# Splitting GpSimd's preparation of a state-space group into two separately ordered steps

## What is computed

```python
def ssd_chunked(x, dt, a, bm, cm):            # 8 groups, 4 heads each, head width 64, state 128
    xdt = x * dt[..., None]
    adt = dt * a ; a_cs = cumsum(adt)
    cb = einsum('bclgn,bcsgn->bcgls', cm, bm)                     # scores of a group
    y_diag = einsum('bcgls,bcgrls,bcsgrp->bclgrp', cb, segsum_exp(adt), xdt)
    ...                                        # the state carries what lies in earlier chunks
def mamba2_mixer(proj, ...):
    z, xbc, dt = split(proj)
    xbc = silu(causal_depthwise_conv(xbc))     # x rows, B and C
    y = ssd_chunked(x, dt, a, B, C) + d_skip * x
    return rmsnorm(y * silu(z))                # by group of 256 columns
```

## Time and profile before

| | |
|---|---|
| three runs, us | 1820.11, 1821.31, 1822.19 (median 1821.31) |
| profiled execution, us | 1821.69 |
| its span, us | 1819.7 |
| granted TensorE clock | 0.998 |
| first state-space layer's groups | about 88 to 300 us of the span |
| second state-space layer's groups | about 1369 to 1581 us |
| table loads of ScalarE | 23, 1.28 us each |

### The profile page before, as it was taken

One profiled execution on the slowest core, in us unless ns is written; L12 is line 12 of the kernel. 1 busy time (PEld: TensorE's weight loads), 2 busy tenths in 40 slices (PEclk: granted clock), 3 DMA queues, 4 the chain that ended last, 5 costly groups with the idle time before them and its releaser, 6 DMA issues.

```text
span 1819.7 us, 25828 instructions
## 1 busy us (share of the span) xinstructions
PE 1792.5 (99%) x9572; PEld 1534.4 (84%) x9572; DVE 1159.0 (64%) x1466; ACT 1000.1 (55%) x1601; POOL 316.3 (17%) x615
## 2 busy tenths in 40 slices
PE   7999999999999999999999999999999999999999
PEld 5999878888887778888888888888899987888887
DVE  5777765566565655566566545655677886556555
ACT  6666764454455666554455645444566666545443
POOL 3443450000003131000001400000144355000000
PEclk9999999999999999999999999999999999999999
DMA  6544434555555433465556445665554443365563
GB/s 230 172 149 153 140 116 139 185 183 189 191 181 183 154 125 126 152 190 193 194 181 214 157 133 176 196 190 190 181 170 152 149 150 128 116 197 184 187 191 131
DMA packets 85272, 305.63 MB, mean 168 GB/s; under 512 B 9632, under 2 KB 11040, under 8 KB 85152
## 3 DMA queue, kind: packets, MB, share of 16 engines
q1 hardware_dynamic: 84576, 302.88, 51.1%
q10 hardware_dynamic: 576, 1.12, 0.2%
HBM read 302.91 MB, written 1.05 MB: 167 GB/s over the span
## 4 chain that ended last, share of the span: by engine, by line
PE 95%; ACT 2%; DVE 2%; issue 1%; DMA 0%; ACTq 0%; DVEq 0%
PE ps L1135 18%; PE ps L1137 18%; PE ps L1136 18%; PE ps L1157 13%; PE ps L1159 7%; PE ps L1146 3%; PE ps L1148 3%; PE ps L1147 3%; PE ps L1291 2%; PE ps L1241 2%; PE ps L1311 2%; PE ps L1175 1%; PE ps L1183 1%; ACT w_hi_t L1336 0%; DVE w_lo_t L1566 0%
## 5 line engine op out<-in xcount | busy, mean ns | idle before, releaser
L1566 DVE TENSOR_TENSOR w_lo_t<-raw,w_hi_t 128x1024 fp32r<-128x1024 f32 x570 | 704.9, 1245 | 465.5 <-ACT w_hi_t L1336 464.1
L1336 ACT ACTIVATE w_hi_t<-raw 128x1024 fp32r<-128x1024 f32 x570 | 598.1, 1059 | 410.3 <-PE ps L1137 162.4
L1157 PE MATMUL ps<-hT,w_hi_t 128*128 128x512 f32 x1024 | 361.6, 397 | 0.0
L1135 PE MATMUL ps<-w_hi_t,act_hi 128*128 128x512 f32 x832 | 328.6, 395 | 0.0
L1137 PE MATMUL ps<-w_hi_t,act_lo 128*128 128x512 f32 x832 | 324.6, 390 | 0.0
L1136 PE MATMUL ps<-w_lo_t,act_hi 128*128 128x512 f32 x832 | 324.0, 389 | 0.0
L1159 PE MATMUL ps<-hT,w_lo_t 128*128 128x256 f32 x1024 | 287.3, 281 | 0.0
L1157 PEld LDWEIGHTS ps<-hT,w_hi_t 128*128 128x128 f32 x1024 | 192.2, 188 | 46.2
L1159 PEld LDWEIGHTS ps<-hT,w_lo_t 128*128 128x128 f32 x1024 | 193.4, 189 | 1.1
L1137 PEld LDWEIGHTS ps<-w_hi_t,act_lo 128*128 128x128 f32 x832 | 156.2, 188 | 33.7
L1135 PEld LDWEIGHTS ps<-w_hi_t,act_hi 128*128 128x128 f32 x832 | 156.2, 188 | 32.1
(11 more groups left out here) (212 smaller groups left out, 2436.5 us busy)
## 6 DMA issues: line engine op xcount, KB each, us to landing
raw<-in_wstream SPq DMA_DIRECT2D x570, 512.0 KB, 3.5
mix<-in_mem SPq DMA_DIRECT2D x4, 256.0 KB, 5.2
x<-in_x SPq DMA_DIRECT2D x1, 1024.0 KB, 9.0
wsT<-in_sgu_wT ACTq DMA_DIRECT2D x1, 512.0 KB, 4.6
sgain<-in_sgu_gain ACTq DMA_DIRECT2D x1, 512.0 KB, 5.6
out<-x SPq DMA_DIRECT2D x1, 512.0 KB, 2.8
out<-x SPq DMA_DIRECT2D x2, 256.0 KB, 2.0
consts_sb<-in_consts SPq DMA_DIRECT2D x1, 384.0 KB, 10.5
```

Of the source, the lines that this page charges most:

```text
L1135: pe.matmul(o, ah, wh[:, n], start=first and c == 0, stop=False)
L1157: pe.matmul(o.rearrange("p (a b) -> p a b", a=2), wh[:, n], hT2[:, :, kt, :], start=first and c == 0, stop=False, skip_group_check=True)
L1336: act.activation(w_hi_t[:, u % RING, :], raw[:, u % RING, :], ACT.Copy).then_inc(w_hi, 1)
L1566: dve.tensor_tensor(w_lo_t[:, u % RING, :], raw[:, u % RING, :], w_hi_t[:, u % RING, :].bitcast(F32), ALU.subtract)\
```

## The change

ssd_prep becomes two steps. ssd_mv makes the masked decays. It waits in the plan for the decay step only, no more for the x rows, and is spawned with no delay right after the previous group's ssd_a. ssd_xd makes the weighed rows. It waits in the plan for the x rows, for ssd_mv of its own group and for ssd_xd of the group before. ssd_a of a group asks for its ssd_mv, ssd_m for its ssd_xd. GpSimd's operations are the same.

```diff
@@ COST
-    "ssd_prep": (0, 0, 0), ...
+    "ssd_mv": (0, 0, 0), "ssd_xd": (0, 0, 0), ...
@@ Plan.ssm
-        def prepare(g, done):
-            while g // 2 not in xs_act or self.decay_act is None:
+        def masked(g, done):
+
+            while self.decay_act is None:
                 yield 1
-            self.step("ssd_prep", g=g, l=l, n=l * SG + g, xs=xs_act[g // 2], done=done)
-            ready[g] = True
+            self.step("ssd_mv", g=g, l=l, n=l * SG + g, done=done)
+            ready["mv", g] = True
+
+        def weighted(g):
+            while g // 2 not in xs_act or ("mv", g) not in ready or (g and ("xd", g - 1) not in ready):
+                yield 1
+            self.step("ssd_xd", g=g, l=l, n=l * SG + g, xs=xs_act[g // 2])
+            ready["xd", g] = True
         ready = {}
 
         def groups():
-            yield from prepare(0, 0)
+            yield from masked(0, 0)
+            self.spawn(weighted(0))
             for g in range(SG):
                 n = l * SG + g
                 yield 1, "ssd_a"
-                while g not in ready or 16 + g // 4 * 4 not in conv or 24 + g // 4 * 4 not in conv:
+                while ("mv", g) not in ready or 16 + g // 4 * 4 not in conv or 24 + g // 4 * 4 not in conv:
                     yield 1
...
                 if g + 1 < SG:
-                    self.spawn(prepare(g + 1, jobs["S", 1].done), 1)
+                    self.spawn(masked(g + 1, jobs["S", 1].done))
+                    self.spawn(weighted(g + 1), 1)
                 yield 1, "ssd_m"
+                while ("xd", g) not in ready:
+                    yield 1
                 self.step("ssd_m", g=g, n=n, jobs=jobs, decay=self.decay_act)
@@ GpSimd
-                elif k == "ssd_prep":
+                elif k == "ssd_mv":
...
                     ins.then_inc(mv_new, 1)
+                elif k == "ssd_xd":
+                    g = s["g"]
+                    pool.wait_ge(rows_in, 16)
                     pool.wait_ge(act_free, s["xs"])
```

More of the change, by code:

```diff
@@ L68 @@
     "evac": (1.2, 0, 0), "conv": (1.0, 2.7, 0), "silu": (1.1, 0, 0), "xs_turn": (1.2, 0, 0.9), "dt": (0, 0.4, 0), "dt_turn": (0.3, 0.7, 0.2),
-    "dt_soft": (0, 0.8, 0), "decay": (0.3, 0, 0.4), "ssd_prep": (0, 0, 0), "ssd_a": (1.5, 0.6, 2.25), "ssd_m": (0, 1.8, 0), "ssd_b": (0.4, 0.85, 2.15),
+    "dt_soft": (0, 0.8, 0), "decay": (0.3, 0, 0.4), "ssd_mv": (0, 0, 0), "ssd_xd": (0, 0, 0), "ssd_a": (1.5, 0.6, 2.25), "ssd_m": (0, 1.8, 0), "ssd_b": (0.4, 0.85, 2.15),
     "ssd_o": (0, 1.7, 0.43), "yg_square": (1.2, 0, 0), "group_scale": (0.8, 0, 0), "d_score": (0, 2.6, 1.3), "d_exp": (2.0, 0, 0), "d_norm": (0, 1.9, 0),
```

## The result

| | before | after |
|---|---|---|
| median of 13 runs each, us | 1820.71 | 1825.09 |
| lowest and highest, us | 1820.11, 1822.19 | 1824.18, 1825.89 |
| profiled execution, us | 1821.69 | 1824.72 |
| its span, us | 1819.7 | 1822.4 |
| granted TensorE clock | 0.998 | 0.999 |

The ratio is 1.0023, with a 95% interval of 1.0015 to 1.0031: 4.4 us slower. The forecast was 1826.0 in a range of 1821 to 1831.

The account below looks back on a forecast made before the run. TensorE, busy 99% of the span, was taken as the bound, so only its waits count. Per layer -0.5 + 0.56 + 2.4 + 0 = +2.5 us, +4.9 for two, gave 1826.0 us, range 1821 to 1831.

Parts of the forecast that it names:

- group 6: masked decays early: At group 6, the 0.93 us wait returns at a transpose; faster VectorE work gains 0.5 us per layer, bounds 0 and 0.7.
- second conv block's silu: At the xs transposes, silu behind the next conv's first half makes TensorE wait 0.75 us, was 0.19: +0.56 per layer.
- group 4: group_r behind masked decays: On GpSimd, group_r runs after group 5's masked decays, so mix transposes wait 2.65 us: net +2.4 per layer.
- groups 0 and 1, GpSimd's weighed rows: At group 0's y products, later weighed rows and E still arrive in time: cost 0, at worst 1.5 us per layer.
- the one without a subtraction beside group_r: Lower bound at group 4: group_r takes 3.4 us with no VectorE subtraction beside it, and the sum is +0.5.
- rival 1: Group_r meets no subtraction and the silu is early enough: +0.2 us a layer, 1821.7 us; chance 0.31.
- the one with stretched masked decays: Upper bound at group 4: four masked decays on GpSimd stretched to 7.0 us, and the sum is +5.4.
- No masked decay is in it: At group 6, ScalarE's chain (z's evacuation, load, E) needs no masked decay, so the transpose still starts at 241.88.
- a margin of 0.3 us: At group 0's y products, the weighed rows and E were expected to fit TensorE's need by 0.3 us.
- Table loads: On ScalarE, 31 loads for 23, 10.3 us more; weight casts 1 to 4 us late cost nothing.
- The rival of a dearer load: A ScalarE table switch costs about 2.66 us, adding 1.4 us a layer at silu and group 0: 1830 to 1831; chance 0.02.
- All that the change could take away is thus 2.05 us a layer: TensorE's waits of 0.93, 0.22, 0.40 and 0.50 us limit the gain to 4.1 us in all, 0.23% of the time.

Follow-up runs that it names:

- experiment 1: The changed kernel, with group 5's masked decays placed behind group_r on GpSimd's queue; 1819.54 us, ratio 0.9991 to the kernel before.
- experiment 4: The kernel before, with the first group_r of each state-space layer computed three times in a row and nothing moved; 1833.30 us, ratio 1.0071.
- experiment 5: The kernel of experiment 1, with the silu of x features 4 to 7 ahead of the next conv's first half; 1817.42 us, ratio 0.9979 to before.
- experiment 6: The kernel of experiment 5, with the last query's two transposes behind group 6's products one unit of weights later; 1814.94 us, ratio 0.9967 to before.
- experiment 2: The kernel before, with only each group's masked decays moved up on GpSimd to right behind the previous group's products; 1818.96 us, ratio 0.9990.
- experiment 3: The changed kernel, but groups from 2 on ask for their x rows as before; groups 0 and 1 keep new places; 1821.97 us, ratio 1.0005 to before.
- experiment 7: The kernel before, with masked decays right behind the last group's products and the last query's two transposes one unit later; 1816.03 us, ratio 0.9973.
- experiment 8: The kernel before, with only the last query's two transposes one unit later and masked decays where they were; 1818.61 us, ratio 0.9988.

## Why the prediction was right

| term, us per layer | forecast | shift measured |
|---|---|---|
| group 6: masked decays early | -0.5 | -0.70 |
| second conv block's silu | +0.56 | +0.58 |
| group 4: group_r behind masked decays | +2.4 | +2.51 |
| groups 0 and 1, GpSimd's weighed rows | 0 | 0 |
| sum of two layers | +4.9 | +4.8 |

The mechanism was right in its main terms. That the total came so near, 1825.09 for 1826.0, owes something to luck: the base of three runs (median 1821.31) was 0.6 us over the 13 runs' 1820.71, the change came out 0.5 us smaller by the medians than forecast (4.4 for 4.9), and rounding had taken 0.2 off. Of the terms, group 6 gave 0.2 us more per layer and group 4 cost 0.1 us more, which partly cancel. One count in the forecast is off without effect: the page has 9572 matmuls, not 8499 rows.

**Group 4**, the main term, holds in each of its steps: masked decays from 186.5 (186.69) to 190.5 (190.78), group_r in 5.35 us with two stretched operations (5.32 us, two), ScalarE's chain 5.37 us (196.22 to 201.53, 5.31). Its wait of 2.65 was split over two transposes, 1.60 and 0.91, which is 2.51. Experiments 1 and 4 show the cause, by taking it away and by making group_r late in the kernel before. Of the bounds, both the one without a subtraction beside group_r (which is also rival 1) and the one with stretched masked decays are out: two small operations were hit, no masked decay was.

**The silu** was forecast to make TensorE wait 0.75 us; it waits 0.73, and experiment 5 removes it by the silu's place alone.

**Group 6**: "No masked decay is in it" (in ScalarE's chain) and "the 0.93 us turn up again as a longer wait there" were right (3.04 us for 3.05), and what goes is VectorE's wait and a little more. The size was off by 0.2 us: it is the price of a wait beyond its row, below. The new wait is 1.60 where I had about 1.3 for the same reason: the last product of group 6 ends 1.45 us behind the start of z's evacuation (242.93 and 241.48) for 2.65 before, 1.20 sooner, although the wait that went had a row of 0.93.

**Groups 0 and 1** had a margin of 0.3 us by my sum; no wait shows there. VectorE's E and TensorE's y products of group 0 in the changed kernel:

```profile
102.70 2.12 DVE L1691 TENSOR_TENSOR E<-E,cbm 128x512 f32<-128x512 f32 x2
...
105.17 1.95 PE L1255 MATMUL ps<-xdt,E 128*128 128x128 f32 x16
```

E was done at 104.82, 0.35 us before TensorE wanted it. This profile lies 0.45 us early from start-up, so in the forecast's times that is 105.27, at the early end of my 105.2 to 106.2; the cover held, but it is as thin as I had it.

**Table loads.** 31 instead of 23, and no cast late enough for TensorE to notice: experiment 6 has all 31 and is the fastest. The rival of a dearer load is out too; the load at 242.58 took 1.28 us and its exponential began 0.01 us behind it. The Trainium skill, page "ScalarE: Activation LUTs", section "What ACT_TABLE_LOAD costs", has about 1.28 us for the load, with which this trace agrees, and about 2.66 us for a switch with its drain, with which it doesn't: 1.29 from the load's start to the next activation.

**A sentence that was wrong**, though the total doesn't show it: "All that the change could take away is thus 2.05 us a layer". Experiment 6 takes 3.26 us a layer from the kernel before and has none of the layer's five waits left, whose rows add up to 2.24 (these four and the 0.19 at xs; two more, 0.8 and 0.2 for the query's norm, are in every kernel and left out). A wait costs more than its row. In the changed kernel's TensorE timeline:

```profile
241.28 0.39 PE L1228 MATMUL ps<-mv_hi,after_r 128*128 128x512 f32 x1
241.51 0.39 PE L1229 MATMUL ps<-mv_lo,after_r 128*128 128x512 f32 x1
```

Matmuls of this size start 0.23 us apart, but each row is 0.39 long. The idle time in brackets counts from the end of such a row, 0.16 us after the next one could have started; and the four transposes behind a wait hold TensorE 0.38 to 0.42 us for 0.35. Together that is about 0.2 us per wait. With it, every kernel's shift per layer follows from its own list of waits, against before (five waits, 2.24 us):

| kernel | waits left in a layer, us | sum + 0.2 each, less before's 3.24 | measured |
|---|---|---|---|
| the change | 0.73, 1.60, 0.91, 1.60 | +2.40 | +2.39, +2.40 |
| experiment 1 | 0.74, 1.60 | -0.50 | -0.49, -0.53 |
| experiment 2 | 0.19, 0.22, 1.61 | -0.62 | -0.68, -0.70 |
| experiment 3 | 0.73, 0.87, 1.61 | +0.57 | +0.80 |
| experiment 4 | 0.19, 4.50, 0.23, 0.93, 0.40, 0.50, and 1.34 for the clock | +6.05 | +6.02, +6.22 |
| experiment 5 | 1.60 | -1.44 | -1.44, -1.46 |
| experiment 6 | none | -3.24 | -3.25, -3.27 |
| experiment 7 | 0.19, 0.22 | -2.43 | -2.47, -2.50 |
| experiment 8 | 0.19, 0.22, 0.93, 0.3 | -0.80 | -0.80, -0.83 |

Experiment 3 misses by 0.2, and so does the second layer of experiment 4; the others agree within 0.1. The 0.2 is fitted to experiments 5 and 6 and to the rows above; the other lines test it.

## What to carry to other kernels

When a step is cut so that one part can run sooner, ask what stands behind that part on its own in-order queue: here masked decays that nobody needed for 32 us went ahead of twelve small operations on which two engines waited, and one condition on the order turned +2.4 us a layer into -0.5. A wait that is removed gains little while another engine's chain ends at the next consumer; move that consumer as well, and the same edit is worth more than twice as much (1.67 us for 0.69). And add up the waits with a fixed price for each (0.2 us here), as the idle time in a pipelined engine's row leaves that part out.

## What the runs showed of the hardware that was not expected

- **The clock behind a wait.** In experiment 4 TensorE waited 4.50 us and then ran at 0.50 (1.2 GHz) until about 202 us; its matmuls took 1.34 us longer per layer, most of which it would otherwise have waited. At about 672 us, behind waits of 1.20 to 1.25 and 0.83 us that all kernels have, the clock was at 0.50 in the profiles of before, experiment 3, 6 and 7, and at 1.00 in those of the change and experiments 1, 2, 4, 5 and 8. It is worth 1.6 to 1.7 us, a third of what the change costs, so a difference of two single profiles can be off by that much.
- **The stretch comes and goes with the execution.** The profiles with it have a mean granted clock of 0.998, those without it 0.999 (experiment 4 aside, 0.997), and the runs of before have both: of the 27, 17 at 0.998 with a median of 1821.61 us and 10 at 0.999 with 1820.35. All 13 runs of the change have 0.999, all 5 of experiment 6 have 0.998. Compared at the same mean clock, the medians come near the shifts of the two layers: the change is 4.7 us over before (shifts +4.8), experiment 2 is 1.4 us under it (-1.38), experiment 6 is 6.5 us under it (-6.52); experiments 1, 3, 5 and 8 agree within 0.5 us. Experiment 7 doesn't: -5.8 at 0.999 and -3.5 at 0.998, for -4.97. The kernel seems to bear on how often the stretch comes; what decides it wasn't tried. The mean clock of a run is the only sign of the stretch outside the profiles.
- **Start-up differs by 1.5 us between kernels.** Before the first state-space layer the same events lay at -0.68 (experiment 5) to +0.85 us (experiment 7) against before, though no edit touches that stretch. Together with the clock this is why I read the terms from shifts within a layer, and why medians some tenths of a microsecond apart say nothing here.
- **GpSimd beside VectorE.** A small GpSimd operation takes 0.20 us, and 1.05 to 1.30 when it meets a subtraction of VectorE; of the twelve of the first group_r, two were hit in the changed kernel, one before.
